# Moving a key head, two low parts and the query-key products in a two-layer encoder kernel

## The chip, the core and the metric

The kernel runs on one core of one Trainium2 chip. The core's five engines are TensorE (PE; its weight loads are listed as PEld), VectorE (DVE), ScalarE (ACT), GpSimd (POOL) and SyncE (SP, which here only starts DMA transfers). The metric is the time of one execution on the device in microseconds, the median of three runs.

## The reference, cut to what matters

One inference step of a streaming encoder of two layers over 512 prompt tokens and 32 sample tokens, width 1024. A layer is a mixer, a cross-attention into 256 memory tokens (4 heads) and a gated feed-forward block. The mixer of layer 0 is half a gated convolution and half a sparse attention: 8 query heads on 2 key heads of 64 features, each query restricted to the keys that an indexer ranks highest. The mixer of layer 1 is a gated recurrence. The parts around the change:

```python
q = _rmsnorm(b_q.reshape(bsz, t, B_HEADS, B_HEAD_DIM), p["b_q_norm"][e])
k_new = _rmsnorm(b_k.reshape(bsz, t, B_KV_HEADS, B_HEAD_DIM), p["b_k_norm"][e])
...
logits = jnp.einsum("btngd,btknd->btngk", qg, k_sel).astype(jnp.float32) * (B_HEAD_DIM ** -0.5)
...
k = _rmsnorm((hm @ w_k).reshape(bsz, m, X_HEADS, X_HEAD_DIM), k_norm)
v = (hm @ w_v).reshape(bsz, m, X_HEADS, X_HEAD_DIM)
```

## The kernel before

All activations stand feature-major: 128 features by 544 tokens (512 + 32). TensorE does every matrix product. A product of full accuracy is made from rounded operands: each operand is split into a high part (rounded, type fp32r) and a low part (what the rounding left), and three rounded products are added, high by high, high by low and low by high. A plain fp32 product is one instruction in the code and two in the trace.

**Weights** come in chunks, most of them 128 output features by 1024 inputs (512 KB). For each chunk SyncE loads WRAW, ScalarE rounds it to WHI (`hi`, line 591), GpSimd subtracts to WLO (`lo`, line 523), and TensorE multiplies (line 1108). There are two buffers of each. The load of chunk c waits until the low part of chunk c-2 is done; the rounding of chunk c waits until TensorE is through with chunk c-2. `ahead(c)` on ScalarE rounds chunk c+2. Chunks in IN_HALVES are rounded and subtracted in halves of 512 columns, and TensorE may start with the first half. Each engine's program is a fixed order written out by hand, and semaphores count what is done.

**Layer 0, input projection.** 29 chunks: nine at the head (indexer, queries, key, value), then for t = 0 to 3 five chunks each, three of the convolution and two of the memory keys. In between VectorE ranks keys (`topk`), scales each query tile (q_out) and the key tile KTT (q_out 5, line 1801). Behind it SyncE stores the new keys, values and indexer keys.

**Attention of layer 0.** `for p in range(PAIRS + 3)`: turn p = 4 j + t makes the two units (key head n = 0 and 1) of query tile j and head group t; tile j has 128, 256, 384 or 512 keys; turn 16 is the sample's. In a turn TensorE makes the query-key products (line 1403), one for each n on its own half of the array's rows (features 0 to 63 and 64 to 127), adds the mask (line 1412), turns the probabilities of turn p-2 (line 1425) and, while p < 7, multiplies two pieces of the memory values' weights (lines 1334 to 1347). VectorE adds the bias and takes the maximum (line 1914), and divides (lines 1927 and 1928). ScalarE makes the exponentials. `attend` multiplies by the values behind each tile.

**Output projection of layer 0 and the memory's key heads.** For output tile m = 0 to 7 VectorE adds the product to X (line 1967), subtracts XL, the low part of the normed tile (line 1647, behind ScalarE's XH), and sums squares (line 1652). Between these `key_sum(m)` and `key_head(m - 3)` norm the memory keys MK: a reciprocal (line 1823) and two products (line 1826) a head, four heads, at m = 3 to 6; each raises mk_out.

**Query projection of the first cross-attention (xq0).** Its eight chunks follow at once. SyncE's order there is written so:

```python
stream(f"xq{l}", 0, 2)
sp.wait_ge(*((mk_out, 4) if l == 0 else (k1_out, 2)))
sp.dma_start(o["mem_k"][l], MK[:]).then_inc(keys_stored, 16)
stream(f"xq{l}", 2)
```

ScalarE rounds the third chunk of xq0 (`ahead(c0)`), takes the norm's square root, and rounds MK (waiting for mk_out 4). VectorE's reciprocal of that root precedes every eviction of the projection.

**Odd layer.** ODD_WORK gives the order of chunks; it ends with gate 6, value 4, value 5, gate 7, value 6, value 7, and then the output projection out_odd. VectorE follows gate m with `scan(m)`, products with the gate (`gated`, line 2208) and low parts for out_odd (`out_low`, lines 2213 and 2215); ScalarE rounds the high parts (`out_high`, lines 1036 and 1038) and evicts the memory values (line 1018). The first chunk of out_odd takes the eight tiles of HL one by one as they come.

Of the kernel before, what the change touches and what calls it, by code (L numbers as in the profile page):

```python
# [24 lines left out]
P = 128  # L25
PROMPT, GAP, SAMPLE = 512, 4, 32
SS = PROMPT
T = SS + SAMPLE
# [4 lines left out]
D, KT = 1024, 8  # L33
# [85 lines left out]
PAIRS = len(UNITS) // 2  # L119
KEY_STORES = 5  # L120
VALUE_TURNS = 7
# [14 lines left out]
FOURTH_SLOTS = {3: 0, T0["up0a"] + 3: 2, T0["up1a"] + 3: 5}  # L136
PAR_FIRST = PAR["bq"][0]

XUNITS = [0, 1, 2, 4, 3]
# [28 lines left out]
def build(nc, a, o, scratch, bands):  # L168

    ctx = ExitStack()  # L170
    with ctx:
        def at(name, shape, dt, offset):
            return nc.alloc_sbuf_tensor_at(name, shape, dt, offset=offset)
# [7 lines left out]
        def pack(start, limit, items):  # L181
# [44 lines left out]
            ("QT", [P, 4, T], F32), ("KTT", [P, KEYS], F32), ("VF", [P, T], F32), ("VT", [P, 6, P], F32),  # L226
            ("SC", [P, 1312], F32), ("MB", [P, 1440], BF16), ("M8", [P, 8], F32)])
        EB = at("EB", [P, 8, 512], F32, M_AT + 2 * 8192)
        BT, OH, RT, MSQ = pack(M_AT + 2 * 8192, S_AT, [("BT", [8, 640], F32), ("OH", [32, 640], F32),
# [32 lines left out]

        PTXHf, MKHf, HHLf = PTXH[:].bitcast(F32), MKH[:].bitcast(F32), HHL[:].bitcast(F32)
        XHf, HHf, MHf = XH[:].bitcast(F32), HH[:].bitcast(F32), [m[:].bitcast(F32) for m in MH]
        WHIf = [w[:].bitcast(F32) for w in WHI]
# [83 lines left out]
        mb_ready, yc_ready, yh_even, yl_even = sem("mb_ready"), sem("yc_ready"), sem("yh_even"), sem("yl_even")  # L349

        qk_done, lg_ready, exp_done, p_ready = sem("qk_done"), sem("lg_ready"), sem("exp_done"), sem("p_ready")
        pt_done, pt_read, pv_done = sem("pt_done"), sem("pt_read"), sem("pv_done")
# [37 lines left out]
        def odd_key_mean(p):  # L390

            return AX[:, 0, :] if p else PS[:, MKT[1][0] % 2, 1, :]

        block = ctx.enter_context(nc.Block())
# [3 lines left out]
        def _(sp):  # L398
# [46 lines left out]
            sp.dma_start(EB[:], bands.rearrange("h p x -> p h x")).then_inc(band_in, 16)  # L445
            n = 0
            stream("in_even", EVEN_HEAD + 4)
            stream("mv0", 0, 2)
            sp.wait_ge(q_out, 5)
            n += store(o["bk"][:, 0:PROMPT], KTT[:, 0:PROMPT])  # L450
            n += store(o["bk"][:, PROMPT:PROMPT + SAMPLE], KTT[:, PROMPT + PAST:KEYS])
            n += store(o["bv"], VF[:])
            n += store(o["bki"][:, 0:PROMPT], KI[0:32, 0:PROMPT])
# [47 lines left out]
            for m in range(KT):  # L501
                if m == KT - 1:
                    sp.wait_ge(last_added, 1)
                    n += store(o["y"][:, m, 0:H], X[:, m, 0:H])
                    sp.wait_ge(evicted, T0["down1b"] + m + 1)
                    n += store(o["y"][:, m, H:T], X[:, m, H:T])
                    continue
                sp.wait_ge(evicted, T0["down1b"] + m + 1)
                n += store(o["y"][:, m, :], X[:, m, :])
            sp.wait_ge(keys_stored, 16 * DEPTH)  # L510
            sp.wait_ge(out_stored, 16 * n)
# [3 lines left out]
        def _(pool):  # L515
# [43 lines left out]
            c = 2  # L559
            while c < N_CHUNKS:  # L560
                if c in (C0["xq0"], C0["xq1"]):
                    cross(int(c == C0["xq1"]))
                    c += 8
                    continue
                halved, piece = c in IN_HALVES, 256 if c in FINE else CHUNK_MAX
                stop = min(x for x in (C0["xq0"], C0["odd"], C0["out_odd"], C0["xq1"], N_CHUNKS) if x > c)
# [16 lines left out]
        def _(act):  # L583
# [158 lines left out]
            def conv_tap(t):  # L742
# [3 lines left out]
                act.activation(UB[:, GS + 2:GS + 4], par("a_hist", 4 * t, 2), ACT.Copy).then_inc(yc_tap, 1)  # L746

            act.wait_ge(std_read, 1)
            act.activation(R2[:], RSTD[:], ACT.Square).then_inc(r2_ready, 1)
            for t in range(A_TILES):  # L750
# [4 lines left out]
                if t == 0:  # L755
                    index_relu(6)
                ahead(i + 1)
                if t == 0:
# [3 lines left out]
                ahead(i + 2)  # L762
                conv_tap(t)
                ahead(i + 3)
                if t == 0:
                    query_std()
                ahead(i + 4)
            conv_high(A_TILES - 1)
# [334 lines left out]
        def _(pe):  # L1103
# [287 lines left out]
            for p in range(PAIRS + 3):  # L1391
                if p in (PAIRS, PAIRS + 1):
                    mixed_part(0, p - PAIRS + 1, p - PAIRS + 2)
                if p < PAIRS:
# [4 lines left out]
                    rows = [(t, slice(0, P))] if j < 4 else [(i, slice(32 * i, 32 * i + 32)) for i in range(4)]  # L1399
                    for n in range(2):  # L1400
                        half = slice(64 * n, 64 * n + 64)
                        for t_, r in rows:
                            ins = pe.matmul(PSB[r, (2 * p + n) % 4, 0:nk], QT[half, t_, q0:q0 + nq], KTT[half, k0:k0 + nk],  # L1403
                                      start=True, stop=j == 0)
                        if j == 0:
                            ins.then_inc(qk_done, 1)
                    if j:
# [227 lines left out]
        def _(dve):  # L1635
# [329 lines left out]
            for m in range(LEN["out_even"]):  # L1965
# [186 lines left out]
            def odd_layer():  # L2152
# [57 lines left out]
                def out_low(m):  # L2210
# [15 lines left out]
                for i, (kind, m) in enumerate(ODD):  # L2226
# [224 lines left out]
```

## Time and profile before

| | |
|---|---|
| median of 3 runs | 1565.43 us (1565.31 to 1565.46) |
| the profiled execution | 1565.22 us, span 1563.3 us |
| TensorE busy | 1547.8 us, 99% of the span |
| VectorE, ScalarE, GpSimd busy | 985.0, 643.2, 669.9 us (63%, 41%, 43%) |
| HBM | 99 GB/s over the span |

Busy time of TensorE includes waits inside its pipeline, so 99% says that it has nearly always an instruction in flight. Where it stands can be seen in the timeline (idle before an instruction, in brackets, with who released it) and in the chain of work that ended last.

### The profile page before, as it was taken

What the parts mean: (1) busy time and instruction counts of PE and PEld (TensorE: products, weight loads), DVE (VectorE), ACT (ScalarE), POOL (GpSimd) and SP (SyncE); (2) the same over time, 40 slices, a digit from 0 to 9 for tenths busy, and PEclk for the clock granted to TensorE, in tenths of its full rate; (3) what the DMA queues carried; (4) which work ended last, traced back from release to release, by engine and by line L of the source; (5) the groups of instructions that cost most, each with busy time, mean ns of one, the idle gap of its engine ahead of it and who ended that gap; (6) DMA issues with size and microseconds to landing.
All of it is one profiled execution on the core that took longest, in us unless ns stands there. A gap on an engine that the chain in (4) does not pass through costs nothing.

```text
span 1563.3 us, 30890 instructions
## 1 busy us (share of the span) xinstructions
PE 1547.8 (99%) x11962; PEld 1488.9 (95%) x11964; DVE 985.0 (63%) x1410; ACT 643.2 (41%) x954; POOL 669.9 (43%) x339
## 2 busy tenths in 40 slices
PE   9999999999999999999999999999999999999999
PEld 7889858998999999999999998999899999999999
DVE  7798885776565564555657879757657552055530
ACT  6332475445433331433335675445543332133321
POOL 3345632461434343434435657554143434343442
PEclk9999999999999999999999999999999999999999
DMA  6343421340322232222323333334122223222222
GB/s 206 130 145 105 129 82 44 106 162 16 120 82 94 86 106 77 81 91 84 107 74 101 107 102 121 109 109 149 39 83 86 90 88 105 68 90 87 92 94 95
DMA packets 43258, 153.91 MB, mean 98 GB/s; under 512 B 5728, under 2 KB 7008, under 8 KB 41896
## 3 DMA queue, kind: packets, MB, share of 16 engines
q1 hardware_dynamic: 43176, 152.75, 29.5%
q8 instruction: 59, 0.97, 0.3%
q14 instruction: 23, 0.19, 0.0%
HBM read 145.53 MB, written 9.30 MB: 99 GB/s over the span
## 4 chain that ended last, share of the span: by engine, by line
PE 84%; DVE 6%; issue 4%; ACT 2%; POOL 2%; DMA 0%; SPq 0%; POOLq 0%; DVEq 0%; ACTq 0%
PE PS L1108 74%; PE AX L1108 3%; POOL WLO L523 2%; DVE TB L2172 1%; DVE SC L1767 1%; ACT PX L864 1%; PE AX L1513 1%; PE AX L1425 1%; PE PS L1403 1%; PE AX L1371 1%; DVE RB L2174 1%; PE AX L1343 1%; PE AX L1344 0%; PE AX L1347 0%; DVE KRC L1823 0%
## 5 line engine op out<-in xcount | busy, mean ns | idle before, releaser
L523 POOL TENSOR_TENSOR WLO<-WRAW,WHI 128x1024 fp32r<-128x1024 f32 (+3 forms) x322 | 637.7, 1992 | 872.1 <-ACT WHI L591 865.3
L591 ACT ACTIVATE WHI<-WRAW 128x1024 fp32r<-128x1024 f32 (+3 forms) x300 | 268.2, 914 | 573.3 <-PE PS L1108 539.3
L1108 PE MATMUL PS<-XH,WHI 128*128 128x272 f32 (+1 forms) x2128 | 443.9, 290 | 4.0 <-DVE XL L1647 1.5
L1108 PE MATMUL PS<-XH,WLO 128*128 128x272 f32 (+1 forms) x2128 | 440.1, 288 | 0.0
L1108 PE MATMUL PS<-XL,WHI 128*128 128x272 f32 (+1 forms) x2128 | 437.7, 287 | 0.0
L1108 PEld LDWEIGHTS PS<-XH,WHI 128*128 128x128 f32 x2128 | 337.2, 188 | 11.5 <-issue 3.7
L1108 PEld LDWEIGHTS PS<-XL,WHI 128*128 128x128 f32 x2128 | 337.2, 188 | 0.0
L1108 PEld LDWEIGHTS PS<-XH,WLO 128*128 128x128 f32 x2128 | 335.3, 188 | 0.0
L1108 PE MATMUL PS<-HH,WHI 128*128 128x272 f32 x1216 | 254.2, 289 | 0.1
L1108 PE MATMUL PS<-HL,WHI 128*128 128x272 f32 x1216 | 252.8, 287 | 0.0
L1108 PE MATMUL PS<-HH,WLO 128*128 128x272 f32 x1216 | 252.8, 287 | 0.0
L1108 PEld LDWEIGHTS PS<-HH,WHI 128*128 128x128 f32 x1216 | 190.8, 188 | 1.5 <-POOL WLO L523 0.5
L1108 PEld LDWEIGHTS PS<-HL,WHI 128*128 128x128 f32 x1216 | 190.5, 188 | 0.0
L1108 PEld LDWEIGHTS PS<-HH,WLO 128*128 128x128 f32 x1216 | 190.4, 188 | 0.0
L1939 DVE TENSOR_TENSOR X<-PS,X 128x544 f32 (+1 forms) x47 | 34.0, 724 | 146.2 <-PE PS L1108 146.2
L1647 DVE SCALAR_TENSOR_TENSOR XL<-X,PR,XH (+1 forms) x40 | 86.3, 2157 | 47.0 <-ACT XH L604 47.0
L2103 DVE SCALAR_TENSOR_TENSOR YB<-GB,PR,YB 128x548 f32<-128x548 f32 x44 | 72.4, 1645 | 52.7 <-ACT YB L932 52.7
L2113 DVE TENSOR_TENSOR HL<-H,HH 128x544 f32 (+1 forms) x44 | 76.5, 1739 | 40.2 <-ACT HH L941 40.2
L937 ACT ACTIVATE GE<-YB 128x548 f32<-128x548 f32 x44 | 29.2, 663 | 113.2 <-DVE YB L2104 113.1
L932 ACT ACTIVATE YB<-GB,PR 128x548 f32<-128x548 f32 x44 | 37.4, 849 | 37.5 <-DVE GB L2101 37.5
L1675 DVE TENSOR_TENSOR GB<-PS,RSTD 128x32 f32<-128x32 f32 x42 | 8.1, 192 | 67.3 <-PE PS L1108 67.2
L941 ACT ACTIVATE HH<-H 128x544 f32 (+1 forms) x44 | 29.1, 661 | 33.7 <-DVE H L2111 33.7
(332 smaller groups left out, 1851.4 us busy)
## 6 DMA issues: line engine op xcount, KB each, us to landing
WRAW<-in_w_in_even SPq DMA_DIRECT2D x28, 512.0 KB, 3.3
WRAW<-in_w_up0a SPq DMA_DIRECT2D x22, 512.0 KB, 3.3
WRAW<-in_w_up0b SPq DMA_DIRECT2D x22, 512.0 KB, 3.3
WRAW<-in_w_up1a SPq DMA_DIRECT2D x22, 512.0 KB, 3.3
WRAW<-in_w_up1b SPq DMA_DIRECT2D x22, 512.0 KB, 3.3
WRAW<-in_w_mv SPq DMA_DIRECT2D x16, 512.0 KB, 3.4
WRAW<-in_w_xq SPq DMA_DIRECT2D x16, 512.0 KB, 3.3
WRAW<-in_w_xo SPq DMA_DIRECT2D x16, 512.0 KB, 3.3
```

Source lines behind the costliest of these rows:

```text
L523: ins = pool.tensor_tensor(WLO[parity][:, w], WRAW[parity][:, w], WHIf[parity][:, w], ALU.subtract)
L591: act.activation(WHI[parity][:, first:last], WRAW[parity][:, first:last], ACT.Copy).then_inc(hi_done, 2 // len(cuts))
L864: act.activation(px[0:nq, i, :], score_bank(s, i // 2)[0:nq, 256 * (i % 2):256 * (i % 2) + 256], ACT.Exp, scale=STAT[:, 1, i:i + 1] if XUN ...
L932: act.activation(YB[:], GB[:, 4:4 + TG], ACT.Identity, scale=par("f_w", f * 3 + (3 * q0 + 2)), bias=par("f_b", f + q0)).then_inc(gconv0, 1)
L937: act.activation(GE[:], YB[:], ACT.Gelu_apprx_tanh).then_inc(gelu_done, 1)
L941: act.activation(HH[:, f, :], H32[:], ACT.Copy).then_inc(hh_ready, 1)
L1108: ins = pe.matmul(dst, w, x, start=first, stop=last)
L1343: pe.matmul(out, MH[l][:, k, tok], WHI[c % 2][:, w], start=k == 0, stop=False)
L1647: dve.scalar_tensor_tensor(XL[:, m, :], X[:, m, :], par(g, m + g0), XHf[:, m, :], ALU.mult, ALU.subtract).then_inc(xl_ready, 1)
L1939: dve.tensor_tensor(halves(X[:, m, :]), PS[:, (t0 + k) % 2, :, 0:H], halves(X[:, m, :]), ALU.add).then_inc(evicted, 1)
L2103: link(dve.scalar_tensor_tensor(YB[:], GB[:, 3:3 + TG], par("f_w", f * 3 + (3 * q0 + 1)), YB[:], ALU.mult, ALU.add))
L2113: dve.tensor_tensor(HL[:, f, :], H32[:], HHf[:, f, :], ALU.subtract).then_inc(hl_ready, 1)
```

## The change

Four edits. (1) The fourth memory key head moves from behind tile 6 of the output projection to behind tile 7. (2) In the odd layer the low parts of value chunks 5 and 7 move from GpSimd to VectorE (`weight_low`), right behind the evictions of gates 6 and 7; GpSimd skips them. (3) In the first attention the query-key products of tiles 0 to 3 are made of three rounded products in place of one plain one; the halves n = 0 and 1 alternate. (4) For these, ScalarE rounds the four query tiles and the key tile of the prompt (QTH, KTH) and GpSimd subtracts their low parts (QTL, KTL) in the place of QT and KTT; KTH takes the place of VF. So the value store goes out before the last sixteen chunks of the input projection are streamed, the prompt's key store goes between the first two loads of value weights, and each has a semaphore of its own. The sample's turn stays plain.

```diff
-            stream("mv0", 0, 2)
+            load(C0["mv0"], a["w_mv0"][0], 1024, C0["mv0"] % 2)
             sp.wait_ge(q_out, 5)
-            n += store(o["bk"][:, 0:PROMPT], KTT[:, 0:PROMPT])
+            sp.dma_start(o["bk"][:, 0:PROMPT], KTT[:, 0:PROMPT]).then_inc(k_stored, 16)
+            load(C0["mv0"] + 1, a["w_mv0"][1], 1024, (C0["mv0"] + 1) % 2)
...
+            sp.wait_ge(evicted, T0["in_even"] + 9)
+            sp.dma_start(o["bv"], VF[:]).then_inc(v_stored, 16)
             stream("in_even", EVEN_HEAD + 4)
...
+            def even_queries_rest(u):
+                pool.wait_ge(q_high, u + 1)
+                pool.tensor_tensor(QTL[:, u, 0:PROMPT], QT[:, u, 0:PROMPT], QTHf[:, u, :], ALU.subtract).then_inc(q_low, 1)
+
+            def even_keys_rest():
+                pool.wait_ge(k_high, 1)
+                pool.wait_ge(k_stored, 16)
+                pool.tensor_tensor(KTL[:, 0:PROMPT], KTT[:, 0:PROMPT], KTHf, ALU.subtract).then_inc(k_low, 1)
+
+            def even_tail():
+                for t in range(1, A_TILES):
+                    for k in range(5):
+                        c = EVEN_TAIL + 5 * (t - 1) + k
+                        lo(c, COLS[c], c % 2, True)
+                        if (t, k) in ROUND_AT:
+                            even_queries_rest(ROUND_AT[t, k])
+                even_keys_rest()
...
+                if c in LOW_ON_VECTOR:
+                    pool.wait_ge(lo_done, c * 2 + 2)
+                    c += 1
+                    continue
...
+            def even_query_round(u):
+                act.wait_ge(q_out, u + 1)
+                act.activation(QTH[:, u, :], QT[:, u, 0:PROMPT], ACT.Copy).then_inc(q_high, 1)
+
+            def even_key_round():
+                act.wait_ge(q_out, 5)
+                act.wait_ge(v_stored, 16)
+                act.activation(KTH[:], KTT[:, 0:PROMPT], ACT.Copy).then_inc(k_high, 1)
...
-                    for n in range(2):
+                    if p == 0:
+                        pe.wait_ge(q_low, 4)
+                        pe.wait_ge(k_low, 1)
+                    for which, (q, k) in enumerate(((QTH, KTH), (QTH, KTL), (QTL, KTH)) if j < 4 else ()):
+                        for n in range(2):
+                            half = slice(64 * n, 64 * n + 64)
+                            ins = pe.matmul(PSB[:, (2 * p + n) % 4, 0:nk], q[half, t, q0:q0 + nq], k[half, 0:nk],
+                                            start=which == 0, stop=which == 2 and j == 0)
+                            if which == 2 and j == 0:
+                                ins.then_inc(qk_done, 1)
+                    for n in range(2 if j == 4 else 0):
...
-                if 3 <= m < XHEADS + 3:
+                if 3 <= m < XHEADS + 2:
                     key_head(m - 3)
+                if m == KT - 1:
+                    key_head(XHEADS - 1)
...
+                def weight_low(c):
+                    dve.wait_ge(lo_done, c * 2)
+                    for n in range(2):
+                        w = slice(512 * n, 512 * n + 512)
+                        dve.wait_ge(hi_done, c * 2 + n + 1)
+                        dve.tensor_tensor(WLO[c % 2][:, w], WRAW[c % 2][:, w], WHIf[c % 2][:, w], ALU.subtract).then_inc(lo_done, 1)
...
                         evict(ODD_C["gate", m], t, t % 2, RG[:, m, :])
+                        if m >= 6:
+                            weight_low(ODD_C["value", 2 * m - 7])
```

## Rows read from the trace of the kernel before

**Rows 1.** The profile's page, part 4: the chain that ended last, by engine

```profile
PE 84%; DVE 6%; issue 4%; ACT 2%; POOL 2%; DMA 0%; SPq 0%; POOLq 0%; DVEq 0%; ACTq 0%
```

**Rows 2.** The chain in order of time: start us, us, what

```profile
182.40 0.42 PE PS L1403 x4
...
184.41 0.24 PE AX L1343
...
225.98 1.06 PE PS L1403 x4
...
235.09 0.87 PE AX L1425 x8
...
302.21 6.02 PE PS L1108 x48
```

**Rows 3.** Busy us in one stretch: PE, PEld, DVE, ACT, POOL

```profile
218.60:230.00 11.40, 11.24 (x58) 5.24 (x60) 10.95 (x43) 9.71 (x26) 0.00 (x0) 1.00 0.00 0
```

**Rows 4.** VectorE's timeline at turn 15 (in brackets: idle before)

```profile
234.92 0.69 DVE L1914 CUSTOM_DVE_ANT_0 LG<-PS,EB 128x512 f32<-128x512 f32 x1 [2.45 <-remote]
```

**Rows 5.** TensorE's timeline at the query projection's first chunk

```profile
300.27 0.52 PE L1108 MATMUL PS<-XH,WHI 128*128 128x272 f32 x2 [1.50 <-DVE XL L1647]
```

**Rows 6.** VectorE's timeline, 283 to 352 us

```profile
289.06 0.88 DVE L1826 SCALAR_TENSOR_TENSOR MK<-MK,PR,KRC 128x256 f32<-128x256 f32 x2
...
291.47 2.21 DVE L1647 SCALAR_TENSOR_TENSOR XL<-X,PR,XH 128x544 fp32r<-128x544 f32 x1 [0.89 <-ACT XH L604]
293.60 0.71 DVE L1652 TENSOR_TENSOR SQA<-SQA,SQ 128x544 f32<-128x544 f32 x1
294.23 1.74 DVE L1823 RECIPROCAL KRC<-KST 128x256 f32<-128x256 f32 x1
296.01 1.90 DVE L1826 SCALAR_TENSOR_TENSOR MK<-MK,PR,KRC 128x256 f32<-128x256 f32 x2
```

**Rows 7.** TensorE's timeline in value chunk 5 of the odd layer

```profile
969.31 0.50 PE L1334 MATMUL AX<-WHI,MH 128*128 128x512 f32 x1 [0.58 <-POOL WLO L523]
```

**Rows 8.** GpSimd, odd layer: low parts of value chunk 5 and gate 7

```profile
965.29 7.42 POOL L523 TENSOR_TENSOR WLO<-WRAW,WHI 128x512 fp32r<-128x512 f32 x4 [1.44 <-ACT WHI L591]
```

**Rows 9.** GpSimd's timeline, 283 to 352 us

```profile
294.84 2.39 POOL L523 TENSOR_TENSOR WLO<-WRAW,WHI 128x1024 fp32r<-128x1024 f32 x1 [1.74 <-ACT WHI L591]
305.41 2.41 POOL L523 TENSOR_TENSOR WLO<-WRAW,WHI 128x1024 fp32r<-128x1024 f32 x1 [8.18 <-ACT WHI L591]
```

**Rows 10.** SyncE's own queue, 296 to 302 us

```profile
297.93 0.34 SPq L478 DMA_DIRECT2D out_mem_k<-MK  x1
298.64 1.60 SPq L403 DMA_DIRECT2D WRAW<-in_w_xq  x2
```

**Rows 11.** ScalarE's timeline, 283 to 352 us

```profile
304.20 1.06 ACT L591 ACTIVATE WHI<-WRAW 128x1024 fp32r<-128x1024 f32 x1 [4.33 <-DMA WRAW<-in_w_xq]
```

**Rows 12.** Busy us and granted clock (the number behind POOL) at the end

```profile
1560.00:1562.00 2.00, 0.59 (x5) 0.38 (x3) 0.44 (x1) 0.00 (x0) 0.00 (x0) 1.00 0.02 8
...
1563.00:1563.30 0.30, 0.00 (x0) 0.00 (x0) 0.00 (x0) 0.00 (x0) 0.00 (x0) 0.65 0.00 0
```

**Rows 13.** Groups of TensorE's instructions by line and form: busy us, mean ns

```profile
L1232 PE MATMUL AX<-SQA 128*128 128x512 f32 x4 | 3.8, 1098 | 1.5 <-DVE SQA L1698 1.5
...
L1598 PE MATMUL PS<-SQA,CST 128*128 128x512 f32 x2 | 1.1, 644 | 0.1
```

**Rows 14.** VectorE's timeline at the end of the odd layer

```profile
977.35 0.73 DVE L1670 TENSOR_TENSOR RG<-PS,RSTD 128x544 f32<-128x544 f32 x1 [1.69 <-PE PS L1108]
...
988.30 0.72 DVE L2213 TENSOR_TENSOR HL<-AX,HH 128x544 fp32r<-128x544 f32 x1 [1.51 <-ACT HH L1036]
```

**Rows 15.** ScalarE's timeline at the end of the odd layer

```profile
985.44 1.16 ACT L591 ACTIVATE WHI<-WRAW 128x512 fp32r<-128x512 f32 x2 [2.07 <-DMA WRAW<-in_w_out_odd]
```

**Rows 16.** Busy time in the input projection's last chunks

```profile
160.00:182.00 22.00, 22.00 (x164) 20.94 (x164) 20.52 (x40) 7.29 (x13) 12.85 (x13) 1.00 0.46 145
```

**Rows 17.** GpSimd's timeline: low part of the first value chunk of layer 0

```profile
174.41 3.65 POOL L523 TENSOR_TENSOR WLO<-WRAW,WHI 128x256 fp32r<-128x256 f32 x4 [0.28 <-ACT WHI L591]
```

More of the change, by code:

```diff
@@ L119 @@
 PAIRS = len(UNITS) // 2
-KEY_STORES = 5
+KEY_STORES = 3
 VALUE_TURNS = 7
@@ L137 @@
 PAR_FIRST = PAR["bq"][0]
+EVEN_TAIL = C0["in_even"] + EVEN_HEAD + 5
+ROUND_AT = {(2, 0): 0, (2, 2): 1, (3, 0): 2, (3, 2): 3}
 XUNITS = [0, 1, 2, 4, 3]
@@ L227, in build @@
             ("SC", [P, 1312], F32), ("MB", [P, 1440], BF16), ("M8", [P, 8], F32)])
+        QTH, QTL = at("QTH", [P, 4, PROMPT], F32R, S_AT), at("QTL", [P, 4, T], F32R, S2)
+        KTL, KTH = at("KTL", [P, KEYS], F32R, S2 + 4 * T * 4), at("KTH", [P, PROMPT], F32R, S2 + 4 * T * 4 + KEYS * 4)
         EB = at("EB", [P, 8, 512], F32, M_AT + 2 * 8192)
@@ L263, in build @@
         PTXHf, MKHf, HHLf = PTXH[:].bitcast(F32), MKH[:].bitcast(F32), HHL[:].bitcast(F32)
+        QTHf, KTHf = QTH[:].bitcast(F32), KTH[:].bitcast(F32)
         XHf, HHf, MHf = XH[:].bitcast(F32), HH[:].bitcast(F32), [m[:].bitcast(F32) for m in MH]
@@ L349, in build @@
         mb_ready, yc_ready, yh_even, yl_even = sem("mb_ready"), sem("yc_ready"), sem("yh_even"), sem("yl_even")
+        q_high, q_low, k_high, k_low = sem("q_high"), sem("q_low"), sem("k_high"), sem("k_low")
+        k_stored, v_stored = sem("k_stored"), sem("v_stored")
         qk_done, lg_ready, exp_done, p_ready = sem("qk_done"), sem("lg_ready"), sem("exp_done"), sem("p_ready")
@@ L392, in odd_key_mean @@
             return AX[:, 0, :] if p else PS[:, MKT[1][0] % 2, 1, :]
+        LOW_ON_VECTOR = {ODD_C["value", 5], ODD_C["value", 7]}
         block = ctx.enter_context(nc.Block())
@@ L446, in _ @@
             n = 0
+            sp.wait_ge(evicted, T0["in_even"] + 9)
+            sp.dma_start(o["bv"], VF[:]).then_inc(v_stored, 16)
             stream("in_even", EVEN_HEAD + 4)
-            stream("mv0", 0, 2)
+            load(C0["mv0"], a["w_mv0"][0], 1024, C0["mv0"] % 2)
             sp.wait_ge(q_out, 5)
-            n += store(o["bk"][:, 0:PROMPT], KTT[:, 0:PROMPT])
+            sp.dma_start(o["bk"][:, 0:PROMPT], KTT[:, 0:PROMPT]).then_inc(k_stored, 16)
+            load(C0["mv0"] + 1, a["w_mv0"][1], 1024, (C0["mv0"] + 1) % 2)
             n += store(o["bk"][:, PROMPT:PROMPT + SAMPLE], KTT[:, PROMPT + PAST:KEYS])
-            n += store(o["bv"], VF[:])
             n += store(o["bki"][:, 0:PROMPT], KI[0:32, 0:PROMPT])
@@ L509, in _ @@
                 n += store(o["y"][:, m, :], X[:, m, :])
+            sp.wait_ge(k_stored, 16)
+            sp.wait_ge(v_stored, 16)
             sp.wait_ge(keys_stored, 16 * DEPTH)
@@ L560, in _ @@
             while c < N_CHUNKS:
+                if c == EVEN_TAIL:
+                    even_tail()
+                    c += 5 * (A_TILES - 1)
+                    continue
                 if c in (C0["xq0"], C0["xq1"]):
@@ L564, in _ @@
                     continue
+                if c in LOW_ON_VECTOR:
+                    pool.wait_ge(lo_done, c * 2 + 2)
+                    c += 1
+                    continue
                 halved, piece = c in IN_HALVES, 256 if c in FINE else CHUNK_MAX
-                stop = min(x for x in (C0["xq0"], C0["odd"], C0["out_odd"], C0["xq1"], N_CHUNKS) if x > c)
+                stop = min(x for x in (EVEN_TAIL, C0["xq0"], C0["odd"], *LOW_ON_VECTOR, C0["out_odd"], C0["xq1"], N_CHUNKS) if x > c)
                 pair, n = COLS[c:c + 2], 0
@@ L756, in _ @@
                     index_relu(6)
+                if t >= 2:
+                    even_query_round(2 * t - 3)
                 ahead(i + 1)
@@ L763, in _ @@
                 conv_tap(t)
+                if t == A_TILES - 1:
+                    even_key_round()
                 ahead(i + 3)
@@ L766, in _ @@
                     query_std()
+                if 1 <= t < A_TILES - 1:
+                    even_query_round(2 * t - 2)
                 ahead(i + 4)
@@ L1399, in _ @@
                     rows = [(t, slice(0, P))] if j < 4 else [(i, slice(32 * i, 32 * i + 32)) for i in range(4)]
-                    for n in range(2):
+                    if p == 0:
[9 more added lines that the diff above has]
+                    for n in range(2 if j == 4 else 0):
                         half = slice(64 * n, 64 * n + 64)
                         for t_, r in rows:
[L1403 to L1406, printed above, removed]
+                            pe.matmul(PSB[r, (2 * p + n) % 4, 0:nk], QT[half, t_, q0:q0 + nq], KTT[half, k0:k0 + nk],
+                                      start=True, stop=False)
                     if j:
```

## The prediction

> **What bounds the kernel now.** I read the page first: TensorE carries 84% of the chain that ended last, VectorE 6%, GpSimd 2% [rows 1]. There is no stage to speed up as a whole; time can only be won where TensorE waits, or where it does something dearly, and it is lost wherever a new wait reaches it. So the next views were the chain in order of time and the timelines around the three places that the diff touches.
>
> In the first attention (182 to 242 us) the query-key products stand on the chain: a pair of them, one for each key head, takes 0.42 us for 128 keys and 1.06 us for 512 [rows 2]. Whether TensorE is really last there changes with the tile. Up to 209 us it is held by its own work, the value products between the turns. From 218.6 to 230 us VectorE is busy 10.95 of 11.40 us [rows 3], without a gap in its timeline; there a shorter product wins nothing. It idles once, 2.45 us before 234.92 us [rows 4], for the product of turn 15.
>
> At the end of the output projection TensorE stands for 1.50 us before 300.27 us, for the last tile of XL [rows 5]. VectorE is what is late [rows 6]: the fourth key head (reciprocal at 294.23, two products at 296.01, done at 297.9) lies ahead of the eviction of tile 7.
>
> In the odd layer TensorE stands in the fifth value chunk, 0.58 us by the row and 0.75 us from start to start, for GpSimd's low part [rows 7]. The seventh value chunk has a second gap of the same size (0.73 us), and the chunk behind each of the two starts 0.23 us late. GpSimd takes 7.42 us for two chunks there [rows 8].
>
> **Part 1, the fourth key head behind the last norm.** Taken away from in front of tile 7: the head's 1.74 + 1.90 us [rows 6]. Tile 7 can be evicted at 294.3, XH follows 0.7 us later, and the subtraction for XL is held by GpSimd's low part until 297.24 [rows 9], as the one of tile 6 was (2.21 us [rows 6]). XL is there at about 297.9; TensorE wants it at 298.6. The gap goes: -1.66 us (1.50 by the row, 1.66 from start to start).
>
> What is late next is the head itself. Behind XL and the sum of squares (0.7) VectorE is free at 298.5; the reciprocal takes 1.74, the two products 0.88 without GpSimd beside them [rows 6]: done at 301.1, where it was done at 297.9. That is 3.2 us later. Two things wait for it by count (mk_out 4). ScalarE's rounding of the keys waits behind other work and has room. SyncE does not: in its program the store of the memory keys stands between the loads of the second and the third weight chunk of the query projection (streams 0 to 2, then the wait, the store, then the rest). Before, the store went out at 297.93, straight after the head, and the load of the third chunk at 298.64 [rows 10]. ScalarE sat 4.33 us until that load had landed and rounded at 304.20 [rows 11]; GpSimd's low part ran from 305.41 to 307.82 [rows 9]; and TensorE, whose second chunk ran from 302.21 to 308.23 [rows 2], started the third without a visible wait. The cover was 0.3 to 0.4 us, no more. Move the head by 3.2 us and the same store, load, rounding and low part end at 311.0. TensorE, which is now 1.7 us early, is through the second chunk at 306.4 and stands for about 4.6 us. Against before the third chunk starts 2.9 us late (311.0 against 308.1). The gain of 1.66 is inside this number. ScalarE's square root and VectorE's reciprocal behind it wait for the same rounding and move by 3.2 us too, so nothing downstream gives it back. Net: **+2.9 us**.
>
> On top comes the clock. Since its first weight chunk TensorE has not stood longer than those 1.5 us, at a granted clock of 1.00. Behind the last product (0.59 us busy from 1560.0 on) it is 0.65 over 1563.0 to 1563.3 [rows 12]: with TensorE at rest it fell to the lower of the two levels (1.2 of 2.4 GHz) there. The stand of 4.6 us is longer than that rest. At the kernel's start the plain products of 512 columns take 1098 ns where the same form later takes 644 [rows 13]; these products run from 1.5 to 6.1 us, so 4.6 us of work passed at the lower level before the clock was up. Price of a fall: 0 below, 4.6/2 = 2.3 us above; I take **+1.8 us**.
> The Trainium skill ("TensorE: Matmul & The Clock Gate", Part 1, The HAM clock gate) says that half rate is the default and that activity releases it, so an idle stretch brings it back; by that rule the fall happens and the sum is the one below, and without it the sum is 1.8 less. The trace's end agrees with it.
>
> **Part 2, low parts of value chunks 5 and 7 on VectorE.** Two pieces of 512 columns each: 0.72 us a piece when GpSimd is quiet (a subtraction of 544 columns, [rows 14]), up to 1.8 when it isn't. VectorE does them right behind the eviction of gates 6 and 7, while GpSimd waits for the next rounding. Gate 6 is evicted by 965.2 and the second half of chunk 5 is rounded by 965.8, so the low part is ready at 965.3 + 2 x 0.7 = 966.7 instead of 969.3. Everything of TensorE behind is 1.0 us earlier then; gate 7 is evicted by 977.2, and chunk 7's low part is ready at 977.2 + 1.4 = 978.6, before TensorE arrives at 979.0. All four gaps go: 0.75 + 0.73 + 0.23 + 0.23 = 1.9 us, the upper bound. What VectorE gets is 2 x 1.4 us more ahead of the scan of tile 7, the gated products and the last low parts, and the output projection's first chunk needs the last of them, HL at 988.30 [rows 14], for its eighth row block, 5.3 us after its start. Before, that HL hung on ScalarE's rounding at 985.44, itself held by a load that GpSimd's low part releases [rows 15]. That load now comes some 3 us earlier, and the rounding hangs on VectorE's product for tile 6, done at 982.7 before; the scan in front of it starts at 978.6 instead of 978.0, so I put it at 983.3: rounding at 983.95, values 1.25, HH 0.6, HL done at 987.6 instead of 989.0. So TensorE gains 1.9 up to that point and gives about 0.5 back. Net: **-1.4 us**; bounds -0.4 (VectorE one microsecond later than I count) and -1.9.
>
> **Part 3, rounded query-key products.** The plain pair takes 0.42 us for 128 and 1.06 for 512 keys, that is 0.21 us fixed plus 1.66 ns a key. That is four columns' time at 2.4 GHz for both heads together: the two row halves run side by side. Three rounded products replace it. A rounded one of 512 columns takes 0.23 us, of 272 columns 0.125 (6.02 us for 48) [rows 2]; 128 columns with a weight load each take 0.11 (0.87 us for 8 transposes, [rows 2]). So 0.21 + 3 x (0.11, 0.12, 0.175, 0.23) = 0.54, 0.57, 0.74, 0.90 for 128, 256, 384, 512 keys, against 0.42, 0.63, 0.85, 1.06: +0.12, -0.06, -0.11, -0.16 a pair. What counts: turns 0 to 2 (+0.36; turn 3 lies in the wait for the first values), 4 to 6 (-0.18), 14 and 15 (-0.32); the others are behind VectorE. Sum -0.1 us, **nothing to measure**. Above: if a rounded product of 128 columns cost what a plain one does (0.21), turns 0 to 2 pay +1.3 in place of +0.36; if rounded halves did not run side by side, the stage pays about +3. Below: all sixteen pairs on the path, -0.8.
>
> The new side work is hidden. ScalarE rounds five tiles of 512 columns at 0.6 us and GpSimd subtracts five at 1.25 us, 3.1 and 6.3 us spread over some 50 us of the input projection, in which ScalarE is busy 7.29 and GpSimd 12.85 of 22 us and TensorE never waits for either [rows 16]. Only the key's stands in front of other work: GpSimd's low part of the first value chunk moves from 174.41 to 175.7 us [rows 17], and TensorE asks for it at 180.5. Without that cover it would cost 1.25. The value store goes out at 77 us, where SyncE's next load is 7 us away, the key store at 168.6 us between loads at 168.2 and 174.2.
>
> **The sum.** 2.9 + 1.8 - 1.4 - 0.1 = +3.2 us. The profiled execution took 1565.22 us (span 1563.3, 1.9 around it), 0.2 less than the median of the runs, 1565.43. That gives 1568.4 for it and **1568.6 us** for the median. A change can be told from none here from 0.2% on, 3.1 us, so the forecast lies on that line.
>
> **Rivals.** (a) The clock stays up through the stand: 2.9 - 1.4 - 0.1 = +1.4, 1566.8 us. For it: nothing in the body of the trace shows a fall. Against: its end does. (b) No late load: if the third chunk's weights were in time, only the gain of part 1 would be left, -1.66 - 1.4 - 0.1 = -3.2, 1562.3 us, faster. The net of part 1 is the head's delay less the 0.3 of cover, down to -1.66 where the load does not wait at all; with a delay under 1.8 us in place of 3.2 the whole change would be no slower. SyncE's order and the 0.7 us between the head's end, store and load [rows 10] speak against. (c) Rounded products are dear, in one of the two ways above: +0.9 to +3, 1569.5 to 1571.7 us. No rounded product below 256 columns and none on half the rows is in this trace. (d) VectorE in the odd layer takes the gain of part 2 back, -0.4: 1569.6 us. For it: VectorE has only 1.69 us of idle time before 977.35 [rows 14], and 1.4 more go in.
>
> **How the numbers follow.** Forecast 0.40, (a) 0.20, (b) 0.10, (c) 0.20, (d) 0.10. The range 1564.5 to 1571.0 leaves out (b) and the dear end of (c), under 2 in 10; the forecast's own range is 1567.3 to 1569.8. Slower by over 0.2% (above 1568.6): half of the forecast, (c) nearly whole, most of (d): 0.46. Within 0.2%: 0.43. Faster: (b) and a little, 0.11.
>
> **What the profile after would show.** Part 1: XL of tile 7 at about 297.9 and no stand before it; the key store on SyncE at 301.1 and the load behind it; TensorE standing 4 to 5 us before the third chunk of the query projection; a granted clock under 1.00 in the 5 us behind that. Part 2: no stand in value chunks 5 and 7, a short one for HL in the first output chunk. Part 3: pairs of 0.5 to 0.9 us where line 1403 stood, no wait for the new low parts. Wrong I am if that stand is under 2 us, if the clock does not move, or if pairs take over 0.7 us at 128 keys.

## The result, and the profile after

The changed kernel took 1570.08 us (median of 9 runs, 1568.05 to 1571.11), the kernel before 1565.40 us in its 9 runs beside them. The ratio is 1.0027, with a 95% interval of 1.0018 to 1.0035: 4.7 us slower. The profiled execution is the longest of the nine, 1571.11 us with a span of 1569.3 (before: 1565.22 and 1563.3), so its trace shows 5.9 us, some 1.2 more than the medians do. Executions more than 1.5% above the fastest of the same kernel (one of run 6 below, two of the kernel before beside the runs) are left out of the ratios and the counts of runs.

First the place where most of it was lost. The chain in order of time through the fourth key head, the store, the load and the third chunk of xq0:

```profile
297.45 0.06 DVE XL L1710
...
300.08 1.67 DVE KRC L1886
...
301.78 0.89 DVE MK L1889 x2
302.69 0.34 SPq L490
...
303.39 5.31 DMA WRAW<-in_w_xq
...
308.77 1.06 ACT WHI L631
...
309.97 2.37 POOL WLO L537
...
312.38 8.87 PE AX L1163 x48
```

Before, the chain in this stretch was TensorE's own work [rows 2]. Now it runs through the key head on VectorE, SyncE, a transfer, ScalarE and GpSimd, and comes back to TensorE 15 us later. The gap of 1.50 us before the projection's first chunk [rows 5] is no longer there, and this is in its place (TensorE's timeline, in brackets the idle time before):

```profile
312.38 0.82 PE L1163 MATMUL AX<-XH,WHI 128*128 128x272 f32 x2 [4.29 <-POOL WLO L537]
```

The third chunk takes 8.87 us. Before it took 6.01:

```profile
308.23 6.01 PE AX L1108 x48
```

The busy times of the changed kernel and its granted clock (the number behind POOL's) say why:

```profile
302.00:308.00 6.00, 6.00 (x49) 5.87 (x47) 0.66 (x2) 0.00 (x0) 0.00 (x0) 1.00 0.75 253
308.00:311.00 3.00, 0.09 (x1) 0.00 (x0) 0.54 (x1) 2.23 (x3) 1.03 (x1) 1.00 0.48 194
311.00:312.00 1.00, 0.00 (x0) 0.00 (x0) 1.00 (x1) 1.00 (x2) 1.00 (x1) 0.68 0.00 0
312.00:318.00 6.00, 5.62 (x25) 5.62 (x26) 4.78 (x5) 4.28 (x5) 5.36 (x4) 0.50 0.27 90
318.00:319.00 1.00, 1.00 (x9) 1.00 (x9) 0.27 (x1) 0.00 (x0) 1.00 (x1) 0.90 0.17 41
```

TensorE rested from 308.1 us; the clock fell during that rest, before any product of the third chunk, and was 0.50 (1.2 of 2.4 GHz) until about 318.

A second fall stands where I had not looked for one, in the first attention. The same windows of the kernel before have 1.00 in each row:

```profile
218.00:219.00 1.00, 0.40 (x2) 0.01 (x1) 0.96 (x5) 0.98 (x4) 0.00 (x0) 1.00 0.02 8
219.00:222.00 3.00, 2.95 (x10) 1.46 (x12) 2.82 (x13) 2.30 (x7) 0.00 (x0) 0.53 0.00 0
222.00:223.00 1.00, 1.00 (x6) 0.24 (x2) 0.93 (x5) 0.47 (x2) 0.00 (x0) 0.69 0.00 0
```

The query-key pairs there, from the chain (before: 0.42 and 1.06 us for 128 and 512 keys [rows 2]). The rows are for 128 keys (two), 256, 384 and 512:

```profile
182.83 0.52 PE PS L1461 x6
...
186.32 0.48 PE PS L1461 x6
...
198.06 0.55 PE PS L1461 x6
...
223.43 0.73 PE PS L1461 x6
...
225.24 0.90 PE PS L1461 x6
```

In the odd layer VectorE's two low parts take 1.29 us each for two pieces, and TensorE's stand in value chunk 5 [rows 7] and its twin in chunk 7 are gone. In the first output chunk TensorE now waits for HL. VectorE's timeline, then TensorE's:

```profile
972.19 1.29 DVE L2287 TENSOR_TENSOR WLO<-WRAW,WHI 128x512 fp32r<-128x512 f32 x2
...
984.13 1.29 DVE L2287 TENSOR_TENSOR WLO<-WRAW,WHI 128x512 fp32r<-128x512 f32 x2
...
994.30 0.72 DVE L2278 TENSOR_TENSOR HL<-AX,HH 128x544 fp32r<-128x544 f32 x1 [0.69 <-ACT HH L1091]
```

```profile
995.08 0.52 PE L1163 MATMUL PS<-HH,WHI 128*128 128x272 f32 x2 [0.59 <-DVE HL L2278]
```

That HL follows HH, ScalarE's rounding of the same tile. Before, HH came right behind ScalarE's own work (first row); now ScalarE has stood 1.26 us for VectorE's product AX when it starts HH (second row):

```profile
987.64 0.62 ACT L1036 ACTIVATE HH<-AX 128x544 fp32r<-128x544 f32 x1
```

```profile
993.64 0.62 ACT L1091 ACTIVATE HH<-AX 128x544 fp32r<-128x544 f32 x1 [1.26 <-DVE AX L2270]
```

So the wait is for VectorE's own work, which runs without a gap from the eviction of gate 7 to AX, the low part of chunk 7 in it.

Laying the start of each TensorE instruction beside the same one of before gives the sum of the profiled execution: +0.3 us up to the attention, +1.2 in its lull, -1.7 at the first chunk of xq0, +4.3 at the third, +2.7 to +2.9 within it, -1.0 and -0.9 in value chunks 5 and 7, +0.7 in the first output chunk: +5.7 to +5.9.

### The profile page after: what moved, and what is told of

Same layout as the page of the kernel before. It is cut to its first block, busy times and chain, and to the rows that moved or that the text cites. A ratio compares the mean times of both kernels' runs of the same rounds, so it can differ in the third digit from the quotient of the medians.

```text
span 1569.3 us, 30912 instructions
## 1 busy us (share of the span) xinstructions
PE 1552.0 (99%) x11996; PEld 1496.2 (95%) x11996; DVE 996.8 (64%) x1414; ACT 643.1 (41%) x959; POOL 668.9 (43%) x340
## 4 chain that ended last, share of the span: by engine, by line
PE 86%; DVE 7%; ACT 3%; issue 2%; DMA 1%; POOL 0%; SPq 0%; DVEq 0%; ACTq 0%; POOLq 0%
PE PS L1163 75%; PE AX L1163 4%; DVE TB L2237 1%; DVE SC L1830 1%; ACT PX L919 1%; PE AX L1576 1%; PE AX L1488 1%; PE AX L1426 1%; DVE RB L2239 1%; PE AX L1398 1%; PE PS L1461 0%; PE AX L1399 0%; PE AX L1402 0%; DVE KRC L1886 0%; DVE HL L2280 0%
## 5 line engine op out<-in xcount | busy, mean ns | idle before, releaser
L537 POOL TENSOR_TENSOR WLO<-WRAW,WHI 128x1024 fp32r<-128x1024 f32 (+4 forms) x318 | 630.0, 1993 | 879.5 <-ACT WHI L631 872.7
L2168 DVE SCALAR_TENSOR_TENSOR YB<-GB,PR,YB 128x548 f32<-128x548 f32 x44 | 63.7, 1448 | 52.5 <-ACT YB L987 52.5
```

The costliest lines, as they stand in the source:

```text
L537: ins = pool.tensor_tensor(WLO[parity][:, w], WRAW[parity][:, w], WHIf[parity][:, w], ALU.subtract)
L2168: link(dve.scalar_tensor_tensor(YB[:], GB[:, 3:3 + TG], par("f_w", f * 3 + (3 * q0 + 1)), YB[:], ALU.mult, ALU.add))
```

## The experiments

Each kernel ran beside the kernel before on the same chip: seven to eleven runs of it. An interval is about 0.1% (1.5 us) to each side, so terms under that are read from the traces. In each set the kernel before took 1565.4 to 1565.6 us. The mean granted clock of each single run is known too, to three digits.

**1. The head back behind tile 6**, all else as changed.

```diff
-                if 3 <= m < XHEADS + 2:
+                if 3 <= m < XHEADS + 3:
                     key_head(m - 3)
-                if m == KT - 1:
-                    key_head(XHEADS - 1)
```

> The changed kernel with the fourth key head back behind tile 6. If the head's place made the store, the third load and the stand of 4.29 us, then the stand and the lower clock behind it go and the 1.66 us gap before XL of tile 7 comes back: 1570.1 - 2.9 (net of part 1) - 2.9 (third chunk back from 8.87 to 6.0 us) = 1564.3 us, some 0.2% under the kernel before (ratio to it 0.999). Rival: the rounded query-key products and the clock fall in the attention carry the loss; then it stays above 1568 us.

Measured: 1564.64 us, ratio 0.9996 (0.9986 to 1.0005). The whole loss goes with the head's place; the rival falls. The lower clock in the attention is still there: 0.81, 0.50 and 0.50 in 218 to 219, 219 to 221 and 221 to 222 us.

**2. The third load first**, the head left behind the last norm.

```diff
                 stream(f"xq{l}", 0, 2)
+                early = 1 - l
+                if early:
+                    load(C0["xq0"] + 2, a["w_xq0"][2], COLS[C0["xq0"] + 2], C0["xq0"] % 2)
                 sp.wait_ge(*((mk_out, 4) if l == 0 else (k1_out, 2)))
                 sp.dma_start(o["mem_k"][l], MK[:]).then_inc(keys_stored, 16)
+                if early:
+                    load(C0["xq0"] + 3, a["w_xq0"][3], COLS[C0["xq0"] + 3], (C0["xq0"] + 3) % 2)
-                stream(f"xq{l}", 2)
+                stream(f"xq{l}", 2 + 2 * early)
```

> The changed kernel with one move in SyncE's order: the load of the third weight chunk of xq0 ahead of the wait for the fourth head and the store of the memory keys. If only that load carries the head's delay to TensorE, the load starts near 298 us, the stand of 4.29 us and the lower clock behind it are gone, and the 1.66 us of part 1 stay won: 1570.1 - 2.9 - 1.66 - 2.9 = 1562.6 us. Rival: the late head reaches TensorE another way too (the reciprocal of the norm's root behind it on VectorE, or the rounding of the keys on ScalarE); then a stand of 1 us or more stays before the third or fourth chunk, and the time is 1564 us or more.

Measured: 1562.57 us, ratio 0.9982 (0.9973 to 0.9991), 7.5 us under the changed kernel. The head is as late as it was, and TensorE waits for nothing of it. SyncE's queue (the third chunk's load, the store, the fourth chunk's load), then ScalarE, then the chain:

```profile
295.26 0.33 SPq L413 DMA_DIRECT2D WRAW<-in_w_xq  x1
303.21 0.34 SPq L493 DMA_DIRECT2D out_mem_k<-MK  x1
303.60 0.43 SPq L413 DMA_DIRECT2D WRAW<-in_w_xq  x1
```

```profile
301.81 1.06 ACT L636 ACTIVATE WHI<-WRAW 128x1024 fp32r<-128x1024 f32 x1 [3.38 <-PE PS L1168]
```

```profile
302.61 6.00 PE PS L1168 x48
308.61 6.01 PE AX L1168 x48
```

The store goes out at 303.21, 5.3 us later than in the kernel before [rows 10], and the third chunk's load at 295.26, 7.9 us ahead of it. The third chunk's rounding no longer waits for a transfer but for TensorE to leave the buffer, at 301.81 in place of 308.77 us. The second and the third chunk run back to back. So the late head reached TensorE through SyncE's order alone.

**3. A run that changed nothing.** Seventeen more products for the stand were put into a branch of `linear` that xq0 does not take, so none was issued.

> The changed kernel with 17 more rounded products of 512 columns on TensorE behind the second chunk of xq0 (about 3.8 us), so that TensorE works where it stood; their results are not used. The third chunk's weights come as late as before, at about 312.3 us. If the lower clock follows from the stand, the granted clock stays 1.00 there, the third chunk takes 6.0 us in place of 8.87, and the whole takes 1570.1 - 2.9 = 1567.2 us. Rival: the lower clock has another cause or costs nothing net (the evictions behind are late anyway); then 1569.5 us or more.

Measured: 1569.36 us (1567.83 to 1571.34), ratio 1.0024 (1.0015 to 1.0034), the stand 4.31 us, the third chunk again at the lower clock. It is a second set of runs of the changed kernel, and says nothing on the theories.

**4. The stand filled**, at the place that TensorE passes. The products' results are not used.

```diff
                     if m == 0:
                         mean_square(norm)
                     if m in (2, 4, 6):
                         head_mean(u0 + m // 2 - 1)
+                    if m == 1 and l == 0:
+                        for _ in range(17):
+                            pe.matmul(AX[:, 3, :], XH[:, 0, 0:P], XH[:, 1, 0:512], start=True, stop=True)
```

> The changed kernel with 17 more rounded products of 512 columns (results not used) behind the second chunk of xq0, at the place that TensorE passes (in the run before this one they stood in a branch that it does not take). They fill some 3.9 of the 4.29 us of the stand; the third chunk still starts near 312.3 us. If the lower clock behind the stand follows from TensorE's rest, the granted clock stays 1.00 from 311 to 319 us, the third chunk takes 6.0 us in place of 8.87, and the whole takes 2.9 us less than the changed kernel (1569.4 to 1570.1 in two sets of runs): 1566.5 to 1567.2 us. Rival: the third chunk's 8.87 us have another cause (the loads or rounding beside it); then its time and the whole stay, 1569 us or more.

Measured: 1568.96 us, ratio 1.0022 (1.0013 to 1.0031). The seventeen products in TensorE's timeline, then the chain behind them:

```profile
307.29 4.12 PE L1618 MATMUL AX<-XH 128*128 128x512 f32 x17
```

```profile
309.59 2.42 POOL WLO L537
312.05 6.28 PE AX L1163 x48
```

The weights came as late, the third chunk took 6.28 us and not 8.87: with TensorE at work the clock stayed up (1.00 in 308 to 320 us). But the median came down by 0.4 to 1.1 us only, where 2.9 was expected. The mean clock rose as it should, to 0.999 or 1.000 in all 11 runs from 0.997 to 0.999 in those of the changed kernel. In this trace a new stand of 0.82 us for GpSimd's low part lies before 974.90 us, which takes back part of it; the rest was not found here. So I repeated the pair without the other parts.

**5 and 6. The head alone, and the head alone with the stand filled** (the edits of the change and of run 4, on the kernel before).

> The kernel before with the fourth key head moved behind the last norm and nothing else. By the traces' terms: gap of 1.66 us gone, third chunk 2.9 us late against before, third chunk 2.9 us longer at the lower clock: 1565.4 + 5.7 = 1571.1 us. With the prediction's own clock term, +1.8: 1570.1 us. Rival: the clock falls only in company of the fall in the attention (rounded products); then the granted clock stays 1.00 behind the stand and the time is 1565.4 + 2.9 = 1568.3 us.

> The kernel before with the fourth head moved and 17 more rounded products of 512 columns (results not used) behind the second chunk of xq0; no other part of the change is in it. Head alone took 1570.7 us, 5.1 over the kernel before, of which the traces put 2.9 on the late third chunk and 2.2 to 2.4 on the lower clock behind the stand. If so, the clock stays 1.00 here and the time is 1565.5 + 2.9 = 1568.4 us. Rival: as in the filled stand of the whole changed kernel, only 0.5 to 1 us comes back, because what follows is late for another reason: 1569.7 us or more.

Measured: head alone 1570.67 us, ratio 1.0032 (1.0020 to 1.0043); filled 1568.99 us, ratio 1.0021 (1.0012 to 1.0030). The chain of each through the third chunk, the windows around it between them:

```profile
308.19 2.36 POOL WLO L523
310.59 8.72 PE AX L1108 x48
```

```profile
309.00:316.00 7.00, 5.41 (x24) 5.41 (x25) 5.78 (x5) 5.49 (x6) 6.36 (x4) 0.51 0.20 75
```

```profile
302.26 5.26 DMA WRAW<-in_w_xq
...
308.81 2.41 POOL WLO L523
311.26 6.29 PE AX L1108 x48
```

```profile
311.00:317.00 6.00, 5.74 (x45) 5.74 (x46) 4.78 (x5) 4.12 (x5) 5.42 (x4) 1.00 0.28 90
```

The head alone costs 5.1 us; filling the stand gives 1.7 back by the medians and 2.4 by the chunk (8.72 to 6.29). What stays, 3.4, is the late load, expected at 2.9. The fall follows from TensorE's rest and needs no company from the attention: the head alone has it with plain products. The intervals of the two ratios overlap, but the runs do not: the seven of the head alone took 1569.92 to 1571.61 us at a mean clock of 0.997 or 0.998, those with the stand filled 1568.51 to 1569.38 us at 0.999 or 1.000.

**7. The low parts alone** (the edits of part 2, on the kernel before).

> The kernel before with only the low parts of value chunks 5 and 7 on VectorE. By the prediction's part 2: -1.4, 1564.0 us; by the trace of the changed kernel (-1.0, -0.9, and 0.7 given back before the first output chunk): -1.2, 1564.2 us. Rival (prediction's d): VectorE takes it back, -0.4, 1565.0 us.

Measured: 1564.68 us, ratio 0.9994 (0.9985 to 1.0003), 0.9 under the 1565.60 beside it. The trace has the two gains of 0.8 to 0.9 us and the wait for HL that gives 0.7 back; there too ScalarE's HH has waited 1.26 us for VectorE's AX:

```profile
988.25 0.52 PE L1114 MATMUL PS<-HH,WHI 128*128 128x272 f32 x2 [0.58 <-DVE HL L2219]
```

**8. Only value chunk 5's low part on VectorE**, on run 10's kernel.

```diff
-        LOW_ON_VECTOR = {ODD_C["value", 5], ODD_C["value", 7]}
+        LOW_ON_VECTOR = {ODD_C["value", 5]}
...
-                        if m >= 6:
+                        if m == 6:
```

> The kernel with plain products, head moved, third load first (1562.84 us), but with only value chunk 5's low part on VectorE; chunk 7's is GpSimd's again. By the trace of the changed kernel chunk 7's move won 0.9 us and the first output chunk gave 0.7 back at once, so it was worth 0.2: 1563.0 us, with the stand before the sixth row block for GpSimd's low part in chunk 7 back and the one for HL gone. Rival: the HL stand comes from chunk 5's low part on VectorE as much as from chunk 7's; then both stands are there and the time is 1563.7 us.

Measured: 1563.08 us against 1562.84. The stand for GpSimd in chunk 7 is back, the one for HL is gone:

```profile
979.78 0.50 PE L1345 MATMUL AX<-WHI,MH 128*128 128x512 f32 x1 [0.56 <-POOL WLO L530]
```

The second move removes a stand and makes the next one. From start to start, the traces of this kernel and of run 10 have it win 0.8 us in chunk 7 and give 0.8 back in the first output chunk. The 0.2 us between the two medians is far under the interval, so what the second move is worth in all is not told from nothing.

**9. The rounded products alone** (parts 3 and 4 of the change, with neither the head nor the low parts).

> Only the rounded query-key products with their side work and store order; the key head and the low parts stay as in the kernel before. By the prediction's part 3: -0.1 us, 1565.3 us. If the clock fall that the changed kernel showed between 219 and 222.5 us belongs to the rounded products, a granted clock under 1.00 shows there again and costs up to 1.2 us: 1565.3 to 1566.6 us. Rival: rounded products are dear (prediction's rival c): 1567 us or more. If the clock stays 1.00 in the attention here, that fall came from something else.

Measured: 1565.66 us, ratio 1.0003 (0.9994 to 1.0012). Its profiled execution, 1564.82 us, has a clock of 1.00 throughout the attention, and TensorE starts xq0 0.5 us earlier than before (299.79 against 300.27 us [rows 5]):

```profile
299.79 0.52 PE L1163 MATMUL PS<-XH,WHI 128*128 128x272 f32 x2 [1.49 <-DVE XL L1710]
```

By what was expected, that would put the fall down to something else. But up to the memory's key heads, behind 283 us, this program is the changed kernel's, so the two traces show two executions of the same attention, one with the fall and one without; and of this kernel's 11 runs, five have a mean clock of 1.000 (median 1565.4 us) and six less (1566.3 us). So the products are not dear. They win about 0.5 us in this trace, where the clock holds, and the median shows nothing of it.

**10. Plain products with the head moved, the third load first and the low parts on VectorE.**

> The kernel before with the fourth head moved, the third load of xq0 ahead of the store, and the low parts of value chunks 5 and 7 on VectorE; the query-key products stay plain. Terms as the traces show them: 1565.4 - 1.7 (gap before XL) - 1.2 (net of the low parts) = 1562.5 us, granted clock 1.00 in the attention. If rounded products in themselves gain 0.5 us or more and lose it to the clock, this one is slower than the padded one by that. Rival: the plain products save the clock fall of 1.2 us that the version with rounded ones (1562.6 us) has, and this is 1561.4 us.

Measured: 1562.84 us, ratio 0.9983 (0.9974 to 0.9992). No different from run 2 with rounded products (1562.57 us); the 1561.4 us that would have been there had the plain products saved a fall in every run were not reached.

**11 and 12. Padding against the clock fall in the attention**, on run 2's kernel: three more pairs a turn, whose results are not used, in all four turns of tile 2, and then in turns 9 and 10 only. The edit of the second:

```diff
+                    for n in [0, 1] * 3 if j == 2 and t in (1, 2) else ():
+                        half = slice(64 * n, 64 * n + 64)
+                        pe.matmul(PSB[:, (2 * p + n) % 4, 0:nk], QTH[half, t, q0:q0 + nq], KTH[half, 0:nk], start=True, stop=True)
```

> The kernel with the third load ahead of the store (1562.6 us), and three more pairs of rounded 384-key products (results not used, 0.52 us a turn) in front of the query-key products of tile 2, where TensorE waits for VectorE and the clock fell from 219.9 to 223.3 us. If the lull's small activity makes the fall, the granted clock stays 1.00 through the attention and the time is 1.2 to 1.4 us less where the fall occurred: 1561.3 us. Rival: the padding reaches the path (VectorE waits for these products) and costs up to 4 x 0.52 us: 1563.5 us or more. No change if the fall comes in few runs only: 1562.6 us.

> The kernel with the third load first and rounded products (1562.6 us, of whose 11 runs four had a mean clock under 1.000), with the three more pairs only in turns 9 and 10, where TensorE stood 1.19 and 0.65 us for VectorE. With them in turns 8 to 11 all runs had a clock of 1.000 but took 1563.45 us; the trace put 0.53 on turn 8 and 0.38 on turn 11. If these two carry the cost, the clock is 1.000 in all or nearly all runs and the time is 1562.5 us or a little less. Rival: the padding costs wherever it stands, 1563.2 us or more; or turns 9 and 10 alone do not hold the clock, and runs at 0.999 and below are there as without padding.

Measured: 1563.45 us, ratio 0.9988 (0.9979 to 0.9997), the mean clock 1.000 in all 11 runs; and 1562.73 us, ratio 0.9985 (0.9976 to 0.9994), 1.000 in 10 of 11. The lull without padding (run 2) and with it (turns 9 and 10):

```profile
219.00:220.00 1.00, 0.40 (x2) 0.40 (x3) 0.93 (x7) 1.00 (x5) 0.00 (x0) 0.83 0.03 8
220.00:223.00 3.00, 3.00 (x12) 1.38 (x12) 2.86 (x13) 2.29 (x8) 0.00 (x0) 0.50 0.00 0
```

```profile
218.00:219.00 1.00, 1.00 (x6) 0.62 (x7) 0.93 (x5) 0.96 (x3) 0.00 (x0) 1.00 0.00 0
219.00:222.00 3.00, 3.00 (x18) 1.28 (x18) 2.83 (x13) 2.24 (x7) 0.00 (x0) 1.00 0.00 0
```

Padding holds the clock. With it in all four turns the median is 0.9 us above run 2's and 0.7 above that with turns 9 and 10 alone; between the two padded traces the span differs by 0.4 us (1560.8 and 1560.4). So turns 8 and 11 seem to lie on the path, but the size is within the intervals. In the two waiting turns no cost can be seen, and the median does not move either: only four of run 2's 11 runs had a mean clock under 1.000.

## Why the prediction was right, and where its terms were off

The sign and the mechanism came out as forecast, the size within the stated range: +3.2 predicted, +4.7 measured, 1570.08 us, but 1.5 above the forecast and above its own range's end, 1569.8. The parts run alone give +5.1, -0.9 and +0.3 (medians), together +4.4. By them most of the missing 1.5 us lies in the late load (0.5 more than forecast), the low parts (0.5 less gained) and the rounded products (0.4 more), each of these differences within its interval; the sizes from the traces are finer.

- **Part 1, the late load** (+2.9): right in each link. The head came 3.2 us later once the 1.6 us that the trace already ran late there are taken off (XL of tile 6 at 293.10 against 291.47 [rows 6]), SyncE sent the store at 302.69, straight after it, and the load behind it, and TensorE stood 4.29 us where 4.6 was expected. The two runs that end it, the head back and the load first, settle the cause. The gap before XL went for 1.7, as predicted. By the medians the term is 3.4 (head alone with the stand filled).
- **The clock** (+1.8, bounds 0 to 2.3): the fall came, as the row of the trace's end had suggested. The term is 1.7 by the medians of the head alone with and without filling, 0.4 to 1.1 in the whole kernel, but 2.4 and 2.9 in the two profiled chunks. The upper bound, 4.6/2, was set too low: it took the time at the lower clock from the 4.6 us of work at the kernel's start, but here the clock was 0.50 from 312 to 318 us, nearly 6 us of work. Between the bounds 1.8 was a choice without a sum of its own; that the medians give 1.7 is luck. Rival (a), no fall, is refuted. The Trainium skill ("TensorE: Matmul & The Clock Gate", Part 1, The HAM clock gate) has the rule that idleness brings back the half rate; runs 4 to 6 agree with it, since products with no use at all kept the chunk at 6.28 and 6.29 us.
- **Part 2** (-1.4): the mechanism was right, the size 0.2 to 0.5 too good. The four gaps went for 1.9 in the trace; the wait for HL gave 0.7 back and not 0.5. The step that was off is the end of that HL, and the path to it. The forecast had it behind ScalarE's rounding of weights and put it 1.4 us earlier than before. It was found at 995.0, that is 988.2 without the 6.8 us that the trace ran late up to there, 0.8 earlier than 989.0. ScalarE was ready 1.26 us before VectorE's AX. In both kernels HL ends 11.7 us behind the start of gate 7's eviction (977.35 [rows 14] and 983.34): the low part's 1.29 us are made up by VectorE's idle time in front of HL (0.69 in place of 1.51) and by a scan of 1.29 in place of 1.83 us. So HL came earlier only by what the move of chunk 5's low part had won. Rival (d), -0.4, is not what the trace shows, though the interval of the low parts alone does not exclude it.
- **Part 3** (-0.1): the price list held, 0.48 to 0.52, 0.55, 0.73 and 0.90 us against 0.54, 0.57, 0.74 and 0.90 predicted. Rival (c) is refuted. The step that failed is the sentence that the products behind VectorE do not count. They do not count as work, but they were what TensorE did in a lull. With less of it the clock fell in the profiled execution (+1.2 us). Where it held, as in the trace of run 9, the products won 0.5, some more than forecast; over run 9's executions the two come to +0.3 in the median, which is not told from nothing.
- **Rival (b)**, no late load, was put at 1562.3 us: the kernel with the load ahead of the store measures 1562.57. It needed one more edit.
- The side work was hidden, as counted: the head back, with all of it, is within the interval of no change.

What stays open: why filling the stand gives 1.7 us back with the head alone and 0.4 to 1.1 in the whole kernel. One new stand was seen in one trace; the difference lies within the intervals. The clock is not what is missing: it came back in all 11 runs of run 4, and yet three of these took 1570.3 to 1570.7 us. Open is also whether the seventeen products cost something of their own.

## What to carry to other kernels

A step that is moved off the critical engine must be followed to all who count it, and the dangerous one is a queue whose order is written down: here a store that nobody hurries for stood ahead of a load with 0.3 us of cover. Ask first whether the queue's order can be changed; with the load ahead of the store the same edit wins 2.8 us where it had lost 4.7. Removing one stand of several in a row is worth little unless the next one's cover is known: the second low part won 0.9 and made the next wait of 0.7, because it stood on the engine that the next step needed.

## What the runs showed of the hardware that was not expected

**A shorter product can lower the clock.** In the lull behind VectorE TensorE already stood 0.65 and 0.53 us with plain products, at 1.00. So it is, with a first stand of 0.52 to 0.66 us, in all six traces with plain products (before, runs 5 to 8 and 10). With the shorter rounded products the stands were 0.94 and 0.65 us and the clock fell to 0.50 right behind them. The first stand was 0.84 to 1.19 us in the five traces that have the fall (the changed kernel and runs 1 to 4) and 0.75 us in the one that has not (run 9). Over all runs, a mean clock of 1.000 was seen in 73 of 92 runs of the kernel before and in 26 of 33 of runs 7, 8 and 10 (plain products, no long stand), in 5 of 11, 3 of 11 and 7 of 11 of the unpadded rounded kernels without a long stand (runs 9, 1 and 2), and in 21 of 22 with padding. The mean does not say where a run fell; three traces (runs 2, 6 and 8) have a fall in the first 11 us as well, with plain and with rounded products alike. Run 8 there:

```profile
7.00:11.00 4.00, 3.63 (x18) 3.63 (x19) 3.33 (x5) 3.78 (x6) 1.75 (x2) 0.62 1.04 410
```

**The price of a rest differs between executions of one kernel.** The nine runs of the changed kernel go with their mean clock: two at 0.999 took 1568.1 and 1568.5 us, two at 0.998 1568.8 and 1569.4, five at 0.997 1570.1 to 1571.1. The mean clock accounts for the 3 us between its fastest and slowest run also by size: 0.002 of 1569 us is 3.1. A term read from one trace (2.9 for the third chunk) can be more than the medians give.
